# One block for the cross attention of prompt and sample tokens: 8 query tiles and 8 sequences taken in pairs

## The chip, the cores and the metric

The kernel runs on one core of a Trainium2 chip. The metric is device time in microseconds (us) of one execution. The engines spoken of are TensorE (PE, with its weight loads as PEld), VectorE (DVE), ScalarE (ACT), GpSimd (POOL) and SyncE (SP, which issues DMAs). TensorE's granted clock is given as a share of 2.4 GHz: 1.00 is 2.4 GHz, 0.50 is 1.2 GHz.

## What is computed

One step of a two-layer decoder in float32: layer 0 mixes with a convolution and latent attention, layer 1 with a state-space scan, and each layer ends in a gated cross attention. Only the cross attention matters here. It runs for 1024 prompt tokens against one memory of 256 tokens that the layer projects itself, and for 8 sequences of 4 sample tokens, each against its own cached memory of 256 tokens.

```python
def cross_attn(h, mk, mv, w_qg, w_o):
    b, t, _ = h.shape
    q, g = jnp.split(h @ w_qg, 2, axis=-1)
    q = q.reshape(b, t, X_HEADS, X_HEAD_DIM)            # 4 heads of 256
    s = jnp.einsum('bthd,bmhd->bhtm', q, mk).astype(F32) * (X_HEAD_DIM ** -0.5)
    p = jax.nn.softmax(s, axis=-1).astype(h.dtype)
    o = jnp.einsum('bhtm,bmhd->bthd', p, mv).reshape(b, t, D_MODEL)
    return (o * jax.nn.silu(g)) @ w_o
...
        xp = xp + rmsnorm(cross_attn(rmsnorm(xp, norm_pre_x[i]), mk, mv, x_w_qg[i], x_w_o[i]), norm_post_x[i])
        xs = xs + rmsnorm(cross_attn(rmsnorm(xs, norm_pre_x[i]), cache_mem_k[i], cache_mem_v[i],
                                     x_w_qg[i], x_w_o[i]), norm_post_x[i])
```

## The kernel before

The program is written engine by engine. A block holds one instruction stream for each engine; streams meet through semaphores inside a block and all engines meet at its end, so blocks run one after the other. `cross_attention` (L2257) runs once for each layer, as a row of such blocks: `memory_keys_values` projects the prompt's memory into KM (keys, transposed) and VM (values); `project` computes the transposed queries QT and the gate SGX = silu(g) for all 1056 tokens; `out_weights` (L453) is a block of SP alone that issues the load of the 4 MB output weights WO and of the gain gb; `cross_prompt`; `cross_sample`; and `out_project` (L463), which multiplies by WO in a three-product split, normalises and adds to X.

`cross_prompt` (L1987) takes the prompt in 8 tiles of 128 queries. For a tile PE computes the scores of 4 heads against 256 keys (`scores`, 8 matmuls of 256 columns, into one of two score tiles xS in PSUM), DVE takes the row maxima (L2044) and scales them (L2046), ACT takes the exponentials with their sums (L2080), DVE normalises (L2051, L2053), PE turns the probabilities into xT (`turn`, 8 transposes), and ACT copies them into HT (L2087), whose old content is no longer needed. After tiles 4 and 7, `values` makes the product with VM for 4 tiles at once, 16 matmuls of 512 columns with VM as weights, and DVE multiplies the result into SGX (L2061).

`cross_sample` (L2109) then takes the 8 sequences one by one. Two slots each hold 1 MB of cached keys (KB, loaded by SP) and values (VB, loaded by POOL), all four in HT; their first loads are issued at the start of this block, since HT was in use until then. For a sequence PE transposes the keys (`keys`, 16 transposes into four PSUM tiles ztp), DVE copies them out (L2195) into KM or VM, PE computes the scores of each head in its own 32-column tile of the array (L2154, both halves of one head in a row), DVE and ACT make the softmax as above, PE turns the probabilities (L2162), and `values` computes the output with VB as 16 full 128 x 128 weights and only 4 moving columns, those of the sequence's own tokens (L2171). DVE multiplies into SGX (L2213).

Matmuls of float32 stand as two records each in the trace, transposes as one. The records name tiles: xS, xT and xO are the prompt's scores, turned probabilities and outputs; ztp, zS, zPT and zO the sample's turned keys, scores, turned probabilities and outputs; WO_part, QT_part, KM_part and SGX_part are views of these buffers in `out_project`.

Of the kernel before, what the change touches and what calls it, by code (L numbers as in the profile page):

```python
# [51 lines left out]
def constants():  # L52
# [35 lines left out]
                            for t in range(16)], 1).astype(np.float32),  # L88
        "c_batch": (np.arange(SMP)[:, None] // TS == np.arange(NB)[None, :]).astype(np.float32),
# [38 lines left out]
def build(nc, A, O):  # L128
# [178 lines left out]
    def project(c, jobs, HT, HH, slots, extra=None, WH=None):  # L307
# [138 lines left out]
    y_w, y_g, y_mm, y_sq, y_ms, y_rs, y_sc, y_x = (sem(n) for n in (  # L446
        "yw_loaded", "ygain_loaded", "y_mm", "y_square", "y_ms", "y_rstd", "y_scaled", "x_updated"))
# [5 lines left out]
    def out_weights(c, W, gain):  # L453

        WO, gb = sb(c, "WO", [P, KT, D]), sb(c, "gb", [P, D])
        with nc.Block() as block:
            @block.sync
            def _(sp):
                sp.dma_start(WO[:], W.rearrange("(k p) n -> p k n", p=P)).then_inc(y_w, 16)
                sp.dma_start(gb[:], gain.partition_broadcast(P)).then_inc(y_g, 16)  # L460
        return WO, gb

    def out_project(YT, weights, WOH, YH, following=None, room=None):  # L463
# [17 lines left out]
        with ExitStack() as c:  # L481
# [55 lines left out]
            def _(act):  # L537
# [122 lines left out]
    s_cload, s_cl2, s_ctp, s_cev = layer_sem("conv_loaded"), sem("conv_w_loaded"), sem("conv_tp"), sem("conv_ev")  # L660
# [48 lines left out]
    s_new, s_sev, s_sout = layer_sem("state_gathered"), sem("state_ev"), sem("state_out")  # L709
# [417 lines left out]
    def mla_prompt(Q, QN, CKV, CKT, KRT, CV, SG, QLS, QRS):  # L1127
# [430 lines left out]
        layer_sem(n) if n != "cache_loaded" else [sem(f"cache_loaded{k}") for k in range(NCH)] for n in (  # L1558
# [347 lines left out]
    def memory_keys_values(l, KM, VM):  # L1906
# [74 lines left out]
        "x_scores", "x_negmax", "x_exp", "x_normed", "x_probs_tp", "x_probs_out", "x_pv", "x_pv_out"))  # L1981
    XSC = XD ** -0.5

    def cross_prompt(l, room, QT, KM, VM, SGX):

        n0 = NQ * l
        with ExitStack() as c:  # L1987
            PB = [sb(c, f"xPB{a}", [P, XH, MEM]) for a in range(2)]

            flat = room[:].rearrange("p k t -> p (k t)")  # L1990
            PT = [flat[:, a * XH * 1024:(a + 1) * XH * 1024].rearrange("p (h q) -> p h q", q=512) for a in range(2)]
            mx, nm, rsum, ri = (sb(c, n, [P, 2, XH]) for n in ("xmx", "xnm", "xrsum", "xri"))
            S = [pb(c, f"xS{a}", (P, XH * MEM)) for a in range(2)]
            TPp = pb(c, "xT", (P, XH * MEM))
            Op = [pb(c, f"xO{a}") for a in range(2)]
            block = c.enter_context(nc.Block())

            @block.tensor
            def _(pe):
                def scores(i):  # L2000
                    if i >= 2:
                        pe.wait_ge(x_ex, XH * (n0 + i - 1))
                    for h in range(XH):
                        for k in range(2):
                            m = nc.tensor.matmul(S[i % 2][:, h * MEM:(h + 1) * MEM], QT[:, 2 * h + k, i * P:(i + 1) * P],  # L2005
                                                 KM[:, 2 * h + k, :], start=k == 0, stop=k == 1)
                    m.then_inc(x_sc, 1)

                def turn(i):
                    pe.wait_ge(x_pn, n0 + i + 1)  # L2010
                    if i:
                        pe.wait_ge(x_te, n0 + i)
                    for h in range(XH):
                        for k in range(2):
                            t = nc.tensor.transpose(TPp[:, (2 * h + k) * P:(2 * h + k + 1) * P],
                                                    PB[i % 2][:, h, k * P:(k + 1) * P], ident[:])
                    t.then_inc(x_tp, 1)

                def values(half):
                    pe.wait_ge(x_te, n0 + 4 * (half + 1))  # L2020
                    for d in range(KT):
                        n = KT * half + d
                        if n >= 2:
                            pe.wait_ge(x_oe, 2 * n0 + n - 1)
                        for k in range(2):
                            m = nc.tensor.matmul(Op[n % 2][:], VM[:, k, d * P:(d + 1) * P], PT[half][:, (d // 2) * 2 + k, :],
                                                 start=k == 0, stop=k == 1)
                        m.then_inc(x_pv, 1)

                scores(0)  # L2030
                for i in range(NQ):
                    if i + 1 < NQ:
                        scores(i + 1)
                    turn(i)
                    if i == 4:
                        values(0)
                values(1)

            @block.vector
            def _(dve):  # L2040
                def maximum(i):
                    v = i % 2
                    dve.wait_ge(x_sc, n0 + i + 1)
                    dve_own.step(dve, nc.vector.tensor_reduce(mx[:, v, :], S[v][:].rearrange("p (h m) -> p h m", h=XH),  # L2044
                                                              AX.X, ALU.max))
                    nc.vector.tensor_scalar(nm[:, v, :], mx[:, v, :], -XSC, None, ALU.mult).then_inc(x_nm, 1)  # L2046

                def normalise(i):
                    v = i % 2
                    dve.wait_ge(x_ex, XH * (n0 + i + 1))  # L2050
                    dve_own.step(dve, nc.vector.reciprocal(ri[:, v, :], rsum[:, v, :]))  # L2051
                    for h in range(XH):
                        ins = nc.vector.tensor_scalar(PB[v][:, h, :], PB[v][:, h, :], ri[:, v, h:h + 1], None, ALU.mult)  # L2053
                    ins.then_inc(x_pn, 1)

                def outputs(half):
                    for d in range(KT):
                        n = KT * half + d
                        dve.wait_ge(x_pv, 2 * n0 + n + 1)
                        part = SGX[:, d, half * 512:(half + 1) * 512]  # L2060
                        nc.vector.tensor_tensor(part, part, Op[n % 2][:], ALU.mult).then_inc(x_oe, 1)  # L2061

                maximum(0)
                for i in range(NQ):
                    normalise(i)
                    if i + 1 < NQ:
                        maximum(i + 1)
                    if i == 4:
                        outputs(0)
                outputs(1)  # L2070

            @block.scalar
            def _(act):
                def exponent(i):
                    v = i % 2
                    act.wait_ge(x_nm, n0 + i + 1)
                    if i >= 2:
                        act.wait_ge(x_tp, n0 + i - 1)
# [18 lines left out]
    def cross_sample(l, room, KM, VM, QT, SGX):  # L2097
# [4 lines left out]
        with ExitStack() as c:  # L2102
# [35 lines left out]
            def _(pe):  # L2138
                def keys(b, s, step, meanwhile=None):
# [8 lines left out]
                    if meanwhile:  # L2148
                        meanwhile()
# [1024 lines left out]
```

## Time and profile before

| | before |
|---|---|
| median of 3 runs | 3289.17 us (3286.83 to 3292.13) |
| profiled execution | 3295.15 us, span 3293.5 us |
| PE busy | 2882.2 us (88%) |
| DVE, ACT, POOL busy | 1488.3, 765.9, 523.6 us |
| layer 0, `cross_prompt` and `cross_sample` | 1187.0 to 1356.3 us |
| layer 1, the same two | 3007.4 to 3177.5 us |

Since blocks follow one another, the time of a block is on the path that sets the end, whatever engine it waits for. Busy time of PE is no measure for the work left in it: records overlap, and at a granted clock of 0.50 the same work lasts twice as long. So this profile is read by block: from the first record of a block to the last, what one round of its loop costs, and at which clock.

### The profile page before, as it was taken

The page shows a single profiled execution, that of the slowest core. Times are in us where ns is not written, and L with a number is a line of the kernel's source. Part 1 is how long each engine was busy: PE and PEld are TensorE (multiplying, and loading weights), DVE is VectorE, ACT ScalarE, POOL GpSimd, SP SyncE. Part 2 cuts the span into 40 slices and gives each one's busy share as a digit, 9 for nine tenths or more (in the row PEclk, how much of TensorE's full clock was granted, in tenths as well). Part 3 has the DMA queues.
Part 4 walks back from the last instruction along what each step waited for, and adds up shares of the span by engine and source line. Part 5 has one row for each costly group of instructions (what it writes and reads, how often), then busy time and mean ns, then how long its engine had stood idle before and what let it go on. Part 6 is the DMA issues. An engine that isn't in the chain of part 4 may idle for free. (4 is left out here: it accounts for less than half of the span.)

```text
span 3293.5 us, 40266 instructions
## 1 busy us (share of the span) xinstructions
PE 2882.2 (88%) x16179; PEld 2278.4 (69%) x16179; DVE 1488.3 (45%) x2523; ACT 765.9 (23%) x1435; POOL 523.6 (16%) x422
## 2 busy tenths in 40 slices
PE   5999895997978998988997798758999977899899
PEld 5997564776758976768997576435555535798576
DVE  4997664663411023345655310557777631102333
ACT  3222352332202221223221211111121210223121
POOL 1012001431202200122121001012212210220011
PEclk9999898997988997798998899778998978899879
DMA  3111004660041114103221221663334103211321
GB/s 106 51 33 44 14 1 174 234 216 4 1 132 53 48 68 153 51 1 87 85 88 61 82 95 46 196 192 96 83 89 113 16 13 115 70 46 71 128 83 47
DMA packets 235057, 270.60 MB, mean 82 GB/s; under 512 B 35926, under 2 KB 190102, under 8 KB 229667
## 3 DMA queue, kind: packets, MB, share of 16 engines
q1 hardware_dynamic: 215074, 179.82, 18.1%
q0 software_dynamic: 16384, 75.77, 6.5%
q10 hardware_dynamic: 3456, 12.98, 1.0%
q8 instruction: 105, 1.72, 0.2%
q14 instruction: 38, 0.31, 0.0%
HBM read 226.64 MB, written 41.28 MB: 81 GB/s over the span
## 5 line engine op out<-in xcount | busy, mean ns | idle before, releaser
L305 PE MATMUL pp<-HH,WS_part 128*128 128x352 f32 x1776 | 575.4, 324 | 0.0
L303 PE MATMUL pp<-HH,WH 128*128 128x352 f32 x1344 | 437.3, 325 | 40.0 <-POOL WS_part L442 40.0
L304 PE MATMUL pp<-HT_part,WH 128*128 128x352 f32 x1344 | 435.3, 324 | 0.0
L305 PEld LDWEIGHTS pp<-HH,WS_part 128*128 128x128 f32 x1776 | 337.4, 190 | 0.0
L303 PEld LDWEIGHTS pp<-HH,WH 128*128 128x128 f32 x1344 | 255.1, 190 | 42.0 <-POOL WS_part L442 42.0
L2717 PE MATMUL OP<-oWO,YT 128*128 128x512 f32 (+1 forms) x576 | 255.9, 603 | 3.3 <-DVE XE L2844 3.3
L304 PEld LDWEIGHTS pp<-HT_part,WH 128*128 128x128 f32 x1344 | 255.2, 190 | 0.0
L442 POOL TENSOR_TENSOR WS_part<-WS,WH 128x1024 fp32r<-128x1024 f32 x56 | 144.1, 2573 | 649.5 <-ACT WH L393 649.5
L2717 PEld LDWEIGHTS OP<-oWO,YT 128*128 128x128 f32 (+1 forms) x576 | 104.9, 184 | 146.4 <-issue 142.8
L2044 DVE TENSOR_REDUCE xmx<-xS 128x4 f32<-128x1024 f32 x16 | 19.5, 1219 | 377.0 <-PE xS L2005 377.0
L993 DVE SCALAR_TENSOR_TENSOR CV<-GXP,cw,CV 128x512 f32<-128x512 f32 x240 | 161.9, 742 | 0.0
L303 PE MATMUL pp<-HH,CK_part 128*128 128x352 f32 x432 | 142.0, 329 | 7.9 <-DVE HT_part L858 7.9
L304 PE MATMUL pp<-HT_part,CK_part 128*128 128x352 f32 x432 | 140.5, 325 | 0.0
L303 PE MATMUL zp<-WZH,HH 128*128 128x512 f32 (+1 forms) x288 | 114.6, 398 | 14.5 <-ACT ZS L2555 14.0
L303 PE MATMUL yp<-QT_part,KM_part 128*128 128x512 f32 (+1 forms) x288 | 115.9, 402 | 12.6 <-DVE WO_part L601 12.6
L304 PE MATMUL yp<-WO_part,KM_part 128*128 128x512 f32 (+1 forms) x288 | 115.6, 401 | 0.0
L305 PE MATMUL yp<-QT_part,SGX_part 128*128 128x512 f32 (+1 forms) x288 | 114.5, 398 | 0.0
L305 PE MATMUL zp<-WZH,HT_part 128*128 128x512 f32 (+1 forms) x288 | 113.9, 396 | 0.0
L304 PE MATMUL zp<-WZ_part,HH 128*128 128x512 f32 (+1 forms) x288 | 113.6, 394 | 0.0
L2698 POOL TENSOR_TENSOR XK<-XK,Db 128x2048 f32<-128x2048 f32 (+1 forms) x9 | 88.1, 9785 | 139.0 <-DVE XD L2870 139.0
L2397 DVE SCALAR_TENSOR_TENSOR oACC<-EP,cwo,oACC 128x1024 f32<-128x1024 f32 x72 | 98.6, 1370 | 9.2 <-DVE oACC L2395 2.4
L2763 PE MATMUL U<-XD,CBt 128*128 128x64 f32 (+1 forms) x576 | 83.4, 318 | 16.5 <-DVE CBt L2876 9.4
(495 smaller groups left out, 5383.3 us busy)
## 6 DMA issues: line engine op xcount, KB each, us to landing
WS<-x_w_qg SPq DMA_DIRECT2D x32, 512.0 KB, 3.9
HT<-cache_mem_k SPq DMA_DIRECT2D x16, 1024.0 KB, 5.1
HT<-cache_mem_v POOLq DMA_DIRECT2D x16, 1024.0 KB, 5.4
CBt<-cum_scratch SPq DMA_DIRECT2D x8, 2048.0 KB, 10.2
xbc_scratch<-oACC ACTq DMA_DIRECT2D x24, 528.0 KB, 2.7
WS<-o_w_in SPq DMA_DIRECT2D x24, 512.0 KB, 3.7
XT<-xbc_scratch SPq DMA_DIRECT2D x8, 1536.0 KB, 7.6
WS<-e_w_in SPq DMA_DIRECT2D x18, 512.0 KB, 4.0
```

The lines of the kernel that those rows point to most:

```text
L303: nc.tensor.matmul(out, wh, xh, start=start, stop=False)
L304: nc.tensor.matmul(out, wh, xl, start=False, stop=False)
L305: return nc.tensor.matmul(out, wl, xh, start=False, stop=stop)
L442: nc.gpsimd.tensor_tensor(WL[:, k % slots, :, :], WS[:, k % slots, :, :], WH[k % 2][:, :, :], ALU.subtract).then_inc(p_lo, 1)
L993: ins = nc.vector.scalar_tensor_tensor(out=out, in0=src, scalar=tap, in1=out, op0=ALU.mult, op1=ALU.add)
L2044: dve_own.step(dve, nc.vector.tensor_reduce(mx[:, v, :], S[v][:].rearrange("p (h m) -> p h m", h=XH), AX.X, ALU.max))
L2397: ins = nc.vector.scalar_tensor_tensor(out=out, in0=src, scalar=tap, in1=out, op0=ALU.mult, op1=ALU.add)
L2698: nc.gpsimd.tensor_tensor(XK[R, :].rearrange("p (h e) -> p h e", h=SH), XK[R, :].rearrange("p (h e) -> p h e", h=SH), Db[R, :].unsqueeze(2 ...
L2717: m = nc.tensor.matmul(OP[hf][0:T, :], YT[:, k, 0:T], WO[:, k, hf * 512:(hf + 1) * 512], start=k == 0, stop=k == NX - 1)
L2763: m = nc.tensor.matmul(U[g % 2][R, e * SP_:(e + 1) * SP_], CB[R, h, R], XD[R, h * SP_:(h + 1) * SP_], start=True, stop=True)
```

## The change

One block, `cross_both`, takes the place of the blocks of `cross_prompt`, `cross_sample` and, in the cross attention, `out_weights`. Its loop takes query tile i together with sequence i.

- PE's order in round i: four times a head's prompt scores (2 matmuls) followed by 4 key transposes of sequence i into a single PSUM tile zT; the turn of tile i-1; the sample scores; four `values` columns of tile i-1; the sample values of sequence i-1; the other four `values` columns; the turn of the sample probabilities.
- Prompt `values` are made for each tile: 16 matmuls of 128 columns instead of 4 of 512 for each tile (16 for 4 tiles), into one PSUM tile xO. The prompt scores have one PSUM tile (before: two).
- Sample scores take the four heads alternately. Sample values now have the probabilities as weights of 32 columns, one column tile of the array for each head, and VB as 256 moving columns: 8 matmuls. They are summed over the sequences in PSUM, where rows of other sequences carry a probability of zero (`own`, a mask of 128 x 8 that DVE multiplies in with the normalisation). After the loop the sum is copied, turned and multiplied into SGX once.
- The scale of the scores goes into QT at the end of the projection, and the maximum comes out negated, so L2046 and L2202 have no successor.
- KB and VB lie in WO's buffer, and the turned keys, probabilities and their copies in HT. WO's four quarters are loaded when the last uses of these slots are done, the last one after the sample values of sequence 7. SP's queue at the block's start holds the keys of sequences 0 and 1, the mask, and gb.
- `out_weights` stays in layer 0's mixer with four DMAs of 1 MB instead of one of 4 MB, and `out_project` waits for the halves of WO separately.

```diff
 def out_project(...):  # ScalarE
-                act.wait_ge(y_w, w0 + 16)
+                act.wait_ge(y_w, 2 * w0 + 32)
                 for rows, cols in quarters:
+                    if rows.start:
+                        act.wait_ge(y_w2, 2 * w0 + 32)
                     nc.scalar.activation(WOH[:, rows, cols], WO[:, rows, cols], ACT.Copy).then_inc(y_wh, 1)
...
+    def cross_both(l, room, KM, VM, QT, SGX, WO, gb):
...
+            @block.sync
+            def _(sp):
+                w = A["x_w_o"][l].rearrange("(k p) n -> p k n", p=P)
+                for b in range(NB):
+                    if b >= 2:
+                        sp.wait_ge(z_tp, 4 * (n0 + b - 1))
+                    sp.dma_start(KB[b % 2], ck[:, b]).then_inc(z_l[b % 2], 16)
+                    if b == 1:
+                        sp.dma_start(own[:], A["c_batch4"]).then_inc(z_m, 16)
+                        sp.dma_start(gb[:], A["norm_post_x"][l].partition_broadcast(P)).then_inc(y_g, 16)
+                for a in range(2):
+                    sp.wait_ge(z_tp, 4 * (n0 + NB - 1 + a))
+                    sp.dma_start(WO[:, 2 * a:2 * a + 2, :], w[:, 2 * a:2 * a + 2, :]).then_inc(y_w, 16)
+                for a in range(2):
+                    sp.wait_ge(z_pv, n0 + NB - 1 + a)
+                    sp.dma_start(WO[:, 4 + 2 * a:6 + 2 * a, :], w[:, 4 + 2 * a:6 + 2 * a, :]).then_inc(y_w2, 16)
...
+                def values(i, a):
+                    pe.wait_ge(x_te, 2 * (n0 + i) + a + 1)
+                    if 2 * i + a:
+                        pe.wait_ge(x_oe, 2 * (n0 + i) + a)
+                    for d in range(4 * a, 4 * a + 4):
+                        for k in range(2):
+                            m = nc.tensor.matmul(OV[:, d % 4 * P:(d % 4 + 1) * P], VM[:, k, d * P:(d + 1) * P],
+                                                 PT[i % 2][:, d // 2 * 2 + k, :], start=k == 0, stop=k == 1)
+                    m.then_inc(x_pv, 1)
+                def sample_keys(b, q):
+                    if q == 0:
+                        pe.wait_ge(z_l[b % 2], 16 * (NB // 2 * l + b // 2 + 1))
+                    if 4 * b + q:
+                        pe.wait_ge(z_te, 4 * (n0 + b) + q)
+                    for k in range(2):
+                        for n in range(2):
+                            t = nc.tensor.transpose(KTp[:, (2 * k + n) * P:(2 * k + n + 1) * P],
+                                                    KB[b % 2][:, n, (2 * q + k) * P:(2 * q + k + 1) * P], ident[:])
+                    t.then_inc(z_tp, 1)
+                def sample_values(b):
+                    pe.wait_ge(z_pe, n0 + b + 1)
+                    pe.wait_ge(z_lv[b % 2], 16 * (NB // 2 * l + b // 2 + 1))
+                    for k in range(2):
+                        for h in range(XH):
+                            m = nc.tensor.matmul(OS[32 * h:32 * h + 32, 0:XD], PZT[b % 2][:, k, 32 * h:32 * h + 32],
+                                                 VB[b % 2][:, k, h * XD:(h + 1) * XD], start=b == 0 and k == 0,
+                                                 stop=b == NB - 1 and k == 1, tile_position=(0, 32 * h), skip_group_check=True)
+                    m.then_inc(z_pv, 1)
+                for i in range(NQ + 1):
+                    for h in range(XH):
+                        if i < NQ:
+                            scores(i, h)
+                            sample_keys(i, h)
+                    if i:
+                        turn(i - 1)
+                    if i < NQ:
+                        sample_scores(i)
+                    if i:
+                        values(i - 1, 0)
+                        sample_values(i - 1)
+                        values(i - 1, 1)
+                    if i < NQ:
+                        sample_turn(i)
...
+                dve.wait_ge(z_m, 16 * (l + 1))
+                for i in range(NQ + 1):
+                    if i < NQ:
+                        for q in range(4):
+                            sample_keys_out(i, q)
+                        maximum(i)
+                        sample_maximum(i)
+                    if i:
+                        outputs(i - 1, 0)
+                    if i < NQ:
+                        sample_normalise(i)
+                        normalise(i)
+                    if i:
+                        outputs(i - 1, 1)
...
-            out_w = out_weights(c, A["x_w_o"][l], A["norm_post_x"][l])
-            cross_prompt(l, HT, QT, KM, VM, SGX)
-            cross_sample(l, HT, KM, VM, QT, SGX)
+            WO, gb = sb(c, "WO", [P, KT, D]), sb(c, "gb", [P, D])
+            cross_both(l, HT, KM, VM, QT, SGX, WO, gb)
```

On PE, a tile of the prompt before stands as scores and turn, with nothing between:

```order
L2005 MATMUL xS_1<-KM,QT 128x256 [waits x_exp]
L2005 MATMUL xS_1<-KM,QT 128x256 x7
L2015 MATMUL xT<-ident,xPB_1 128x128 [waits x_probs_out,x_normed]
L2015 MATMUL xT<-ident,xPB_1 128x128 x7
L2005 MATMUL xS_1<-KM,QT 128x256 [waits x_exp]
```

On PE after, one round of the loop (its first two key quarters left out) holds the prompt's scores and key transposes in turn, then the rest of both kinds of tokens:

```order
L2052 MATMUL xS<-KM,QT 128x256 x2
L2088 MATMUL zT<-ident,WO 128x128 [waits z_k_out]
L2088 MATMUL zT<-ident,WO 128x128 x3
L2065 MATMUL xT_1<-ident,HT 128x128 [waits x_normed]
L2065 MATMUL xT_1<-ident,HT 128x128 x7
L2099 MATMUL zS<-HT,QT 32x256 [waits z_probs_out,z_k_out]
L2099 MATMUL zS<-HT,QT 32x256 x7
L2076 MATMUL xO<-HT,VM 128x128 [waits x_probs_out]
L2076 MATMUL xO<-HT,VM 128x128 x7
L2114 MATMUL zO<-WO,PZT_1 32x256 [waits memv_slot0,z_probs_out]
L2114 MATMUL zO<-WO,PZT_1 32x256 x7
```

Every key quarter now waits until DVE has emptied the one zT tile, and between two such quarters PE has a head's prompt scores to do.

On SP, at the start of the cross attention's block of the changed kernel, what the queue holds:

```order
L2025 DMA WO<-cache_mem_k 128x2x1024 x2
L2027 DMA xown<-c_batch 128x8
L2028 DMA gb<-norm_post_x 128x1024
L2025 DMA WO<-cache_mem_k 128x2x1024 [waits z_k_tp] x6
L2032 DMA WO<-x_w_o 128x2x1024 [waits z_k_tp] x2
L2035 DMA WO<-x_w_o 128x2x1024 [waits z_pv] x2
```

And on DVE of the changed kernel, its first instructions in that block:

```order
L2161 COPY HT<-zT 128x512 [waits z_k_tp,z_mask]
L2161 COPY HT<-zT 128x512 [waits z_k_tp] x3
L2143 TENSOR_REDUCE xnm<-xS 128x4 [waits x_scores]
L2167 TENSOR_REDUCE znm<-zS 128x1 [waits z_scores]
```

DVE's first copy waits for the mask, which stands in SP's queue behind 2 MB of keys.

## Rows read from the trace of the kernel before

**Rows 1.** Timeline, block borders, layer 0: start us, duration us, engine, line, what
```profile
1184.86 0.46 ACT L2270 ACTIVATE SGX<-pp 128x352 f32<-128x352 f32 x1 [3.35 <-PE pp L305]
...
1187.02 7.14 PE L2005 MATMUL xS<-KM,QT 128*128 128x256 f32 x32 [2.19 <-PEq L456]
...
1356.12 0.19 DVE L2213 TENSOR_TENSOR SGX<-SGX,zO 128x32 f32<-128x32 f32 x1 [8.26 <-PE zO L2171]
...
1357.57 7.29 ACT L548 ACTIVATE QT_part<-WO 128x2048 fp32r<-128x2048 f32 x4
...
1362.40 0.77 PE L303 MATMUL yp<-QT_part,KM_part 128*128 128x512 f32 x1 [6.32 <-DVE WO_part L601]
```
**Rows 2.** Timeline, layer 1: first and last record of the two blocks
```profile
3007.36 5.81 PE L2005 MATMUL xS<-KM,QT 128*128 128x256 f32 x18 [2.54 <-PEq L456]
...
3177.27 0.19 DVE L2213 TENSOR_TENSOR SGX<-SGX,zO 128x32 f32<-128x32 f32 x1 [8.27 <-PE zO L2171]
```
**Rows 3.** Stretches: length, busy PE, PEld, DVE, ACT, POOL (records), PEclk, DMA share, GB/s
```profile
1187.00:1266.30 79.30, 67.33 (x256) 44.23 (x256) 32.08 (x72) 24.13 (x73) 0.00 (x0) 0.94 0.15 60
1266.30:1356.40 90.10, 83.02 (x528) 70.61 (x528) 31.45 (x72) 7.58 (x24) 5.82 (x8) 0.68 0.52 187
```
**Rows 4.** Timeline, one prompt tile in the first of the two blocks
```profile
1195.44 1.22 DVE L2044 TENSOR_REDUCE xmx<-xS 128x4 f32<-128x1024 f32 x1
1195.58 1.09 PE L2015 MATMUL xT<-ident,xPB 128*128 128x128 f32 x8 [1.42 <-DVE xPB L2053]
1196.51 3.62 PE L2005 MATMUL xS<-KM,QT 128*128 128x256 f32 x16
...
1197.63 0.47 ACT L2080 ACTIVATE xPB<-xS,xnm 128x256 f32<-128x256 f32 x1
...
1199.81 1.14 DVE L2053 TENSOR_SCALAR xPB<-xPB,xri 128x256 f32<-128x256 f32 x4
```
**Rows 5.** Timeline, one sequence in the second block
```profile
1296.39 3.65 PE L2145 MATMUL ztp<-ident,HT 128*128 128x128 f32 x16
...
1302.23 4.38 PE L2171 MATMUL zO<-PZT,HT 128*128 x32
...
1306.47 3.65 PE L2145 MATMUL ztp<-ident,HT 128*128 128x128 f32 x16
```
**Rows 6.** Stretches of half a microsecond inside that sequence
```profile
1304.50:1305.00 0.50, 0.50 (x7) 0.50 (x6) 0.00 (x0) 0.00 (x0) 0.00 (x0) 1.00 0.04 16
...
1306.00:1306.50 0.50, 0.50 (x4) 0.50 (x4) 0.00 (x0) 0.00 (x0) 0.00 (x0) 0.50 0.00 0
```
**Rows 7.** Layer 0's latent attention on sample tokens: timeline, then the stretch around it
```profile
599.71 1.53 PE L1653 MATMUL KTp<-ident,HT 128*128 128x128 f32 x12
601.07 1.02 PE L1660 MATMUL Sc<-RTs,QD 128*128 128x512 f32 x2
...
603.34 1.08 PE L1686 MATMUL Op<-HT,PCT 128*32 128x128 f32 x32
604.24 1.04 PE L1666 MATMUL Sc<-QN,DTt_part 128*32 128x512 f32 x8
605.21 0.98 PE L1653 MATMUL KTp<-ident,HT 128*128 128x128 f32 x7
...
598.00:606.00 8.00, 8.00 (x113) 5.63 (x106) 4.79 (x10) 2.52 (x5) 3.57 (x7) 1.00 0.67 250
```
**Rows 8.** Layer 1's scan, full-width weights with 64 moving columns: timeline, then its stretch
```profile
2229.16 7.06 PE L2763 MATMUL U<-XD,CBt 128*128 128x64 f32 x32 [1.67 <-DVE Y L2892]
...
2229.00:2236.00 7.00, 6.84 (x32) 6.87 (x33) 1.30 (x3) 0.00 (x0) 0.38 (x1) 0.50 0.00 0
```
**Rows 9.** Start of the sample block: timeline, then landing of the 16 key loads
```profile
1271.41 3.41 PE L2145 MATMUL ztp<-ident,HT 128*128 128x128 f32 x16 [5.86 <-DMA HT<-cache_mem_k]
1272.57 0.69 DVE L2195 COPY KM<-ztp 128x512 f32<-128x512 f32 x1 [6.29 <-PE ztp L2145]
...
DMA to landing us min/median/max: 4.7/5.1/9.3
```

More of the change, by code:

```diff
@@ L1995, in cross_prompt @@
[L1995 to L2070, printed above, removed]
@@ L2092, in build @@
[L2092 to L2108 removed]
+            KBT = [flat[:, a * 2048:(a + 1) * 2048].rearrange("p (k m) -> p k m", m=MEM) for a in range(2)]
@@ new lines, in scores, with turn @@
+                def scores(i, h):
+                    if h == 0 and i:
+                        pe.wait_ge(x_ex, n0 + i)
+                    for k in range(2):
+                        m = nc.tensor.matmul(S[:, h * MEM:(h + 1) * MEM], QT[:, 2 * h + k, i * P:(i + 1) * P],
+                                             KM[:, 2 * h + k, :], start=k == 0, stop=k == 1)
+                    if h == XH - 1:
+                        m.then_inc(x_sc, 1)
+                def turn(i):
+                    pe.wait_ge(x_pn, n0 + i + 1)
+                    for a in range(2):
+                        if i:
+                            pe.wait_ge(x_te, 2 * (n0 + i - 1) + a + 1)
+                        for h in (2 * a, 2 * a + 1):
+                            for k in range(2):
+                                t = nc.tensor.transpose(TPp[a][:, (2 * (h % 2) + k) * P:(2 * (h % 2) + k + 1) * P],
+                                                        PB[i % 2][:, h, k * P:(k + 1) * P], ident[:])
+                        t.then_inc(x_tp, 1)
@@ L2176, in _ @@
-                keys(0, 0, 0)
-                keys(1, 1, 0, lambda: turned(0, 0))
-                values(0, 0, 0)
-                with loop(pe, 0, NB // 2 - 1) as j:
-                    for s in range(2):
-                        keys(2 * j + 2 + s, s, j + 1, lambda: turned(2 * j + 1 + s, 1 - s))
-                        pe.wait_ge(z_oe, n0 + 2 * j + s + 1)
-                        values(2 * j + 1 + s, 1 - s, j + s)
-                turned(NB - 1, 1)
-                pe.wait_ge(z_oe, n0 + NB - 1)
@@ new lines, in sample_turned @@
+                def sample_turned(b):
+                    act.wait_ge(z_pt, n0 + l + b + 1)
+                    if b >= 2:
+                        act.wait_ge(z_pv, n0 + b - 1)
+                    nc.scalar.activation(PZT[b % 2][:], SS[:, MEM:2 * MEM].rearrange("p (k q) -> p k q", k=2), ACT.Copy).then_inc(z_pe, 1)
+                for i in range(NQ + 1):
+                    if i:
+                        turned(i - 1, 0)
+                        turned(i - 1, 1)
+                    if i < NQ:
+                        exponent(i, 0)
+                        exponent(i, 1)
+                        sample_exponent(i)
+                        exponent(i, 2)
+                        exponent(i, 3)
+                        sample_turned(i)
```

221 lines of the change are left out of this document (95 added, 126 removed).

## The prediction

> **What bounds the kernel now.** Blocks follow one another, so I first read the borders in the timeline. In layer 0 the projection's last gate copy ends at 1185.32 us (1184.86 + 0.46), the prompt block's first matmul starts at 1187.02, and the sample block's last multiplication ends at 1356.31 [rows 1]: 171.0 us. In layer 1 the two blocks take 170.1 us [rows 2], with the same 1.7 us ahead of them 171.8. The change touches these 342.8 us and hardly more.
>
> Then the busy time by stretch. The prompt block takes 79.3 us at a granted clock of 0.94, the sample block 90.1 us at 0.68 [rows 3]. Neither is full in its own way. In a prompt tile PE has 0.93 us of transposes and 3.6 us of scores and otherwise waits for the chain maximum, four exponentials, normalisation [rows 4]: latency. In a sequence PE is never idle, one comes every 10.08 us [rows 5], but the output matmuls with 4 moving columns hold it for 4.2 us, and behind them the clock has fallen from 1.00 to 0.50 [rows 6], so that 16 transposes take about 3.4 us.
>
> **The new round, PE's work.** At clock 1.00, start to start:
> - prompt scores, 16 records: 3.45 us (3.62 with the last one's tail) [rows 4];
> - turn of a tile, 8 transposes: 0.93 [rows 4];
> - 16 key transposes: 12 take 1.36 us, so 0.113 each, 1.8 [rows 7];
> - sample scores: 16 records of 256 columns in alternating 32-column tiles. The nearest row has 8 of 512 columns, as many columns in all: 0.97 [rows 7];
> - sample values are the same shape: 0.97;
> - prompt values: 32 records of 128 columns with full-width weights. This shape doesn't stand in the trace by itself. Below, a transpose has such a weight load and 128 columns in 0.113 us; above, load and matmul would not overlap, 0.107 + 0.107 us. With 64 columns at clock 0.50, 32 records take about 6.9 us, 0.215 each, although the columns alone would add 0.107 to a load of 0.214 if the two excluded one another [rows 8]. They overlap, so I take the transpose's 0.113: 3.6 us;
> - turn of the sample probabilities: 0.23.
>
> Sum 12.0 us.
>
> A rule speaks against the many shapes in a round. The Trainium skill, TensorEngine Tiling (Array Packing), Key Properties, states that changing the tiling mode drains TensorE. A round has four such changes, a sequence before had two. The row shows little of it: the 8 tiled records of rows 7 take 0.97 us where a quarter of 8 x 0.43 (twice a 256-column record's 0.216) is 0.86, so at most 0.11 for a drain, 0.22 us more a round and some 4 us in all; 0.97 already holds half of that.
>
> **The new round, waits.** I walk through one from PE's first score at 0. A head's scores and a key quarter take 0.86 + 0.45; 0.3 us after a quarter's transposes DVE starts its copy, which takes 0.69 (four transposes at clock 0.50 take 0.85 from 1271.41, the copy starts at 1272.57) [rows 9]. The next head's scores hide 0.86 of the 1.05 us, so each of three quarters waits 0.2: the last ends at 5.8, its copy at 6.8. The turn of the tile before fills 5.8 to 6.7; the sample scores wait 0.1, and end at 7.8; four value columns until 9.6, sample values until 10.6, the other value columns wait 0.1 for the one xO tile and end at 12.5, the sample's turn at 12.7. So a round takes **12.8 us**.
>
> Is anything else later? DVE takes the maximum (1.22) from 6.8 to 8.0, the sample's to 8.5, ACT's five exponentials of 0.45 us run from 8.1 to 10.5 with the wait for the sample's maximum hidden. The next scores need the one score tile empty: 10.5 against 12.8, slack 2.3. DVE normalises until 12.6 (0.7 for the output, 0.5 and 1.3 for the two), and is free when the next quarter comes at 14.4. DVE works 8.1 us of the round, ACT about 5. The DMAs bring 2 MB a round, less dense than the 2 MB in 10.08 us before [rows 5]; a slot has over 10 us for a median landing of 5.1 us [rows 9]. The removed L2046 and L2202 (under 0.2 us each) lie in hidden time: nothing.
>
> **First and last round.** The keys are fetched only when the block starts, as before; PE waited 5.86 us and went on at 4.9 us after the issue, at half clock (3.41 us for 16 transposes) [rows 9]. Now DVE's first copy also waits for the mask, which is queued on SP behind the second sequence's keys. The slowest key load, the second of a pair, landed after 9.3 us [rows 9]; it is issued 0.4 us after the first, so the mask comes at about 10.2 and PE's second quarter starts at 10.95. Who waits: PE, with everything behind it. Three more head scores and quarters, partly at half clock, end near 15.8, the copy at 16.8, maxima at 18.5, exponentials at 20.5: the first round takes **21 us** (16.5 if the mask comes with the first keys). The last one: turn 0.9, copy by ACT, values from 1.5 to 3.3, sample values to 4.3, values to 6.2, output 7.2, copy, turn, two small multiplications: **8.6 us**.
>
> WO's last quarter is issued at 4.6 in that round and lands at 9.7 by the median. ACT needs it about 3.3 us after the block's end at 8.6 (0.3 us border, then the gate's split and one quarter; this is 1357.57 + 1.9 against 1356.31 in rows 1). The slack is 2.2 us, so nothing; with a landing of 9.3 us it costs 2.0 us a layer.
>
> **The sum.** A layer: 0.3 (an ordinary border, as at 1356.31; SP's block of its own is gone) + 21 + 7 x 12.8 + 8.6 = 119.5 us. Two layers 239.0 against 342.8: 103.8 us less. The mixer's three more DMA issues, about 0.43 us each in a block of SP alone, give back 1.3. Against the profiled execution: 3295.15 - 102.5 = 3192.7. That execution lies 6.0 us above the median of the runs, so for the median **3186.7 us**.
>
> Bounds: a round of 12.0 (no wait) and a first round of 16.5 give 5.6 + 4.5 us less a layer: 3166. If each of PE's 11 waits in a round costs a full hand-off of 0.3 us, a round takes 15.3; with 3 us more in the first and 2 us for WO that is 22.5 us more a layer, 3232.
>
> **Rivals.**
> - *Hand-offs bound, not PE.* One score tile, one xO and one zT tie PE, DVE and ACT together. For it: in the prompt block such a chain sets the time already [rows 4]. Against: the slack of 2.3 us. Rounds of 15.3 us: 3222 to 3235.
> - *The value columns cost twice*, 0.213 us a record: 3.2 us x 8 rounds x 2 layers more, 3238. Against it stands rows 8.
> - *The clock stays as in the sample block.* At 0.68 a round takes 12.0 / 0.68 + 0.8 = 18.4 us, 39 us more a layer: 3265. For it: half of the work comes from there. Against: before the fall PE did matmuls of 4 columns, which are gone, and a stage of transposes, tiled and full matmuls runs at 1.00 [rows 7]. The Trainium skill, TensorE: Matmul & The Clock Gate, Part 4, holds that transposes don't count as busy for the clock; the trace doesn't bear that out at 601.07, where they fill most of the time before and the clock is 1.00.
> - *Slower than before.* The one mechanism that reaches this is the clock: with rounds of (171.4 - 0.3 - 29.6) / 7 = 20.2 us all gain is gone, that is from a mean clock of 12.0 / 19.4 = 0.62 downwards. The place is the loop, whose every round holds a few waits of PE; in the first round PE idles over 3 us twice, and a fall like that of rows 9 would have to last. At 0.50 throughout, rounds of 24.8 us give 84 + 9 us more a layer: 3373.
> - *It doesn't overlap*: PE's in-order stream makes the pair of a tile and a sequence as long as the two were. 79.3 / 8 + 10.1 = 20.0 us [rows 3, 5] a round, and the time is unchanged. The walk excludes it.
>
> **How the numbers follow.** Forecast 0.72 (3166 to 3222), hand-offs 0.10, value columns 0.04, clock at 0.68 0.08, slower 0.03, no overlap 0.01, below 3166 0.02. The range takes the first two: 3166 to 3235. A measurement tells about 0.2% (6.6 us) from no change. Faster 0.96, within 0.2% 0.01, slower 0.03.
>
> **What the changed profile would show.** Starts of the maximum L2143 every 12.8 us at a clock of 0.95 or more; DVE's first copy near 10 us after the block's start, released by a DMA; 32 xO records in 3.6 us; no idle time of ACT in `out_project` released by WO's load. I am wrong if L2143 comes every 15 us with PE idle before xS (hand-offs), if xO's records stand 0.2 us apart, or if PEclk in the loop is under 0.8.

## The result, and the profile after it

| | before | after |
|---|---|---|
| median of 4 runs each, same chip | 3290.65 us (3286.83 to 3293.24) | 3190.12 us (3189.32 to 3191.76) |
| profiled span | 3293.5 us | 3187.7 us |
| layer 0, gate's end to `out_project` | 171.3 us | 122.3 us |
| layer 1, the same | 172.4 us | 119.5 us |

The ratio is 0.9698, with a 95% interval of 0.9684 to 0.9712: faster, 3.4 us above the forecast of 3186.7. The last two rows of the table are taken from the end of the projection's last gate copy to ACT's first split of SGX in `out_project` (KM_part), so that the border is in; they are used below for every kernel. Together they lost 101.9 us. One single run of the kernel before, beside the last pair of experiments, took 4331.69 us at a mean clock of 0.63 and is left out of every comparison.

The page of the changed kernel begins with its span and the busy times:

```profile
span 3187.7 us, 40235 instructions
PE 2791.4 (88%) x16311; PEld 2213.6 (69%) x16311; DVE 1485.6 (47%) x2481; ACT 767.1 (24%) x1451; POOL 520.1 (16%) x422
```

PE's share is 88% as before, so it tells nothing of the change. The stretches tell more (length, busy PE, PEld, DVE, ACT, POOL, granted clock, DMA share, GB/s): layer 0's whole block, its steady rounds, and the beginning of its second round.

```profile
1189.40:1311.10 121.70, 109.07 (x850) 85.13 (x850) 61.12 (x123) 32.16 (x105) 5.83 (x8) 0.92 0.49 177
1220.00:1300.00 80.00, 80.00 (x683) 62.73 (x684) 47.67 (x94) 26.49 (x90) 4.29 (x6) 1.00 0.48 170
1211.50:1217.50 6.00, 6.00 (x22) 4.90 (x20) 2.41 (x7) 0.38 (x1) 0.00 (x0) 0.56 0.00 0
```

Before, the two stretches ran at 0.94 and 0.68 [rows 3]. Now 80 us of rounds run at 1.00, and PE's records leave no gap there. The borders of the block, beside [rows 1], from the timeline of layer 0:

```profile
1188.67 0.46 ACT L2256 ACTIVATE SGX<-pp 128x352 f32<-128x352 f32 x1 [3.35 <-PE pp L306]
...
1189.44 1.10 PE L2052 MATMUL xS<-KM,QT 128*128 128x256 f32 x4 [0.81 <-PEq L2260]
...
1302.75 1.04 PE L2065 MATMUL xT<-ident,HT 128*128 128x128 f32 x8
...
1310.66 0.48 DVE L2195 TENSOR_TENSOR SGX<-SGX,zS 128x128 f32<-128x128 f32 x2 [0.53 <-PE zS L2136]
...
1311.44 1.06 ACT L546 ACTIVATE KM_part<-SGX 128x1024 fp32r<-128x1024 f32 x1 [6.97 <-PEq L2000]
...
1312.41 7.29 ACT L553 ACTIVATE QT_part<-WO 128x2048 fp32r<-128x2048 f32 x4
```

ACT's split of WO (L553) follows its split of SGX without a gap: the late load of WO costs nothing. The last round, from 1302.75 to 1311.14, takes 8.4 us.

One steady round in the timeline, to be read beside [rows 4] and [rows 5]; it goes from the score at 1233.28 to the one at 1245.95:

```profile
1233.12 1.21 DVE L2143 TENSOR_REDUCE xnm<-xS 128x4 f32<-128x1024 f32 x1
1233.28 1.07 PE L2099 MATMUL zS<-HT,QT 128*32 128x256 f32 x16
1234.28 2.05 PE L2076 MATMUL xO<-HT,VM 128*128 128x128 f32 x16
...
1236.26 1.07 PE L2114 MATMUL zO<-WO,PZT 128*32 128x256 f32 x16
...
1237.26 2.05 PE L2076 MATMUL xO<-HT,VM 128*128 128x128 f32 x16
...
1239.15 0.38 PE L2106 MATMUL zS<-ident,PZ 128*128 128x128 f32 x2
...
1239.37 1.03 PE L2052 MATMUL xS<-KM,QT 128*128 128x256 f32 x4
...
1240.67 1.03 PE L2052 MATMUL xS<-KM,QT 128*128 128x256 f32 x4
1240.87 0.69 DVE L2161 COPY HT<-zT 128x512 f32<-128x512 f32 x1 [0.83 <-PE zT L2088]
1241.62 0.66 PE L2088 MATMUL zT<-ident,WO 128*128 128x128 f32 x4
1242.11 1.03 PE L2052 MATMUL xS<-KM,QT 128*128 128x256 f32 x4
...
1244.98 1.04 PE L2065 MATMUL xT<-ident,HT 128*128 128x128 f32 x8
...
1245.79 1.22 DVE L2143 TENSOR_REDUCE xnm<-xS 128x4 f32<-128x1024 f32 x1
1245.95 1.07 PE L2099 MATMUL zS<-HT,QT 128*32 128x256 f32 x16
```

The round takes 12.67 us. Start to start, it is sample scores 1.00, values 1.98, sample values 1.00, values 1.89, the sample's turn 0.22, four heads with their key quarters 5.61, the tile's turn 0.97. The first quarter of the four takes 1.30, those that wait for DVE's copy 1.44 (1240.67 to 1242.11); the 0.14 us between them shows only from start to start, since the modelled ends of the records cover it. The two column-tiled groups take 1.00 us each at four tiles of 32 columns; the output by 4 moving columns took 4.2 us in [rows 5].

The first round, beside [rows 9], on PE and DVE:

```profile
1194.24 1.12 PE L2088 MATMUL zT<-ident,WO 128*128 128x128 f32 x4 [3.69 <-DMA WO<-cache_mem_k]
1195.15 1.92 PE L2052 MATMUL xS<-KM,QT 128*128 128x256 f32 x4
1200.37 0.69 DVE L2161 COPY HT<-zT 128x512 f32<-128x512 f32 x1 [192.09 <-DMA xown<-c_batch]
1201.12 1.11 PE L2088 MATMUL zT<-ident,WO 128*128 128x128 f32 x4 [4.05 <-DVE HT L2161]
...
1211.58 1.91 PE L2052 MATMUL xS<-KM,QT 128*128 128x256 f32 x4
...
xown<-c_batch SPq DMA_DIRECT2D x1, 4.0 KB, 10.0
```

DVE's copy waits for the mask (xown), which lands 10.0 us after its issue (the last row is from the DMA issues of that stretch: size, us to landing). PE stands for 4.05 us behind it. The scores of the next heads run at half clock (1.92 us for 4 records instead of 1.03), and so does the start of the second round at 1211.58, at 0.56 in the stretch above.

### The profile page after: what moved, and what is told of

Its sections match the earlier page's. It is cut to its first block and busy times, and to the rows that moved or that the text cites. A ratio compares the mean times of both kernels' runs of the same rounds, so it can differ in the third digit from the quotient of the medians.

```text
span 3187.7 us, 40235 instructions
## 1 busy us (share of the span) xinstructions
PE 2791.4 (88%) x16311; PEld 2213.6 (69%) x16311; DVE 1485.6 (47%) x2481; ACT 767.1 (24%) x1451; POOL 520.1 (16%) x422
## 5 line engine op out<-in xcount | busy, mean ns | idle before, releaser
L2161 DVE COPY HT<-zT 128x512 f32<-128x512 f32 x64 | 44.2, 691 | 437.1 <-DMA xown<-c_batch 383.6
L1732 DVE COPY QN<-KTp 128x512 f32<-128x512 f32 x128 | 82.7, 686 | 27.6 <-PE KTp L1658 27.6
## 6 DMA issues: line engine op xcount, KB each, us to landing
CBt<-cum_scratch SPq DMA_DIRECT2D x8, 2048.0 KB, 10.1
```

Source lines behind the costliest of these rows:

```text
L1732: nc.vector.tensor_copy(KTs[:, r, :], KTp[r % 3][:]).then_inc(d_kte, 1)
L2161: nc.vector.tensor_copy(KBT[b % 2][:, 2 * q:2 * q + 2, :], KTp[:].rearrange("p (k m) -> p k m", k=2))\
```

## Experiments

All of them change `cross_both`, but for one that starts from the kernel before. The kernel before was run beside each; its single runs there lie between 3275.6 and 3308.6 us, so small differences are read from the profiled stages as well.

**The mask ahead of the keys**

```diff
             def _(sp):
+                sp.dma_start(own[:], A["c_batch4"]).then_inc(z_m, 16)
                 for b in range(NB):
...
                     if b == 1:
-                        sp.dma_start(own[:], A["c_batch4"]).then_inc(z_m, 16)
```

> The mask is loaded first on SP's queue, ahead of both key loads; nothing else differs from the changed kernel (3190.1 us). Theory (DVE's first copy waits for the mask, and the mask for the second sequence's keys): the first copy starts about 6 us after the block's start instead of 10.9, the first round takes 17.5 us instead of 22.1, the rounds after it 12.68 as before; 3181 us. Rival (the copy waits, but the second sequence's keys or the half clock decide when the second round starts): the first copy moves and the second round's first scores don't; 3190 us.

Measured: 3178.43 us (3170.74 to 3187.84, 6 runs), ratio to before 0.9655 (0.9622 to 0.9687). From its timeline, the first round:

```profile
1182.15 1.10 PE L2052 MATMUL xS<-KM,QT 128*128 128x256 f32 x4 [0.81 <-PEq L2260]
1187.38 1.07 PE L2088 MATMUL zT<-ident,WO 128*128 128x128 f32 x4 [4.13 <-DMA WO<-cache_mem_k]
...
1188.57 0.69 DVE L2161 COPY HT<-zT 128x512 f32<-128x512 f32 x1 [186.52 <-PE zT L2088]
...
1189.96 1.05 PE L2088 MATMUL zT<-ident,WO 128*128 128x128 f32 x4
...
1194.54 1.21 DVE L2143 TENSOR_REDUCE xnm<-xS 128x4 f32<-128x1024 f32 x1
```

The copy is released by PE's transposes. The mask now lands 1.5 us after its issue instead of 10.0, as the trace of its loads tells:

```profile
DMA to landing us min/median/max: 1.5/1.5/1.5
```

The first maximum starts 12.4 us after the first score instead of 18.2 (12.8 instead of 17.9 in layer 1). The next maximum comes 11.6 and 11.7 us later, as changed 12.8 and 10.2: this span depends on how much of the second round's start runs at half clock, here 2.6 us in layer 0 and a little more in layer 1, as changed 5.1 and none. The layers take 115.4 and 115.8 us, 10.6 us less together than the changed kernel's 241.8. The wait for the mask is a cost of its own, on the path of the block. The first copy starts 6.4 us after the first score, as the theory said (about 6).

Since the intervals of the two kernels' ratios touch, they were run once more, side by side on one chip:

> The changed kernel itself, beside the version with the mask first on the same chip, since the times of one kernel on different chips differ by more than the effect in dispute. By the theory its first maximum stands 18.3 to 18.6 us after the loop's first score and the median is 9 to 11 us above the version with the mask first; if that version's gain was a matter of the chip or of the run, the two agree within 3 us.

> The mask's load stands ahead of the keys on SP's queue, all else is the changed kernel, run on the same chip. By the theory (one latency in each layer's first round, 5.3 us a layer) 9 to 11 us less than the changed kernel here, ratio to the kernel before 0.003 lower than the changed kernel's. Rival: the clock's course elsewhere gives it back, under 5 us less.

Measured: 3187.24 us (3182.51 to 3193.98, 5 runs; ratio 0.9684, 0.9655 to 0.9712) as changed and 3182.73 us (3172.93 to 3192.25, 6 runs; 0.9667, 0.9640 to 0.9695) with the mask first. In the profiled runs the first maximum stands 17.5 and 18.4 us after the first score as changed, 13.0 and 12.7 us with the mask first; the layers take 240.5 and 231.9 us together, the spans are 3180.8 and 3171.3. So the stages differ by 8.7 us, a little under what was expected (in layer 0 as changed the clock came back earlier than in the first profile, by the fourth head's scores), and the profiled spans by 9.5, but the medians by only 4.5: less than the theory asked for, within the rival's "under 5 us", and inside the scatter of 11 and 19 us between single runs. The rival's mechanism isn't seen in the two profiled runs, which differ by only 0.8 us outside the two stages. What is shown is the gain in the stage, twice, in both layers. In the whole time it isn't shown clear of noise: the medians differ by 4.5 us here and by 11.7 in the first set, and in both sets the intervals of the ratios overlap.

**The turn among the key quarters**

```diff
                         if i < NQ:
                             scores(i, h)
+                        if i:
+                            turn(i - 1, h)
+                        if i < NQ:
                             sample_keys(i, h)
-                    if i:
-                        turn(i - 1)
```

(`turn` takes two transposes of one head at a time.)

> The turn of a prompt tile is cut into four pairs of transposes, one behind each head's scores and ahead of the key quarter, so that PE has 1.09 us of work instead of 0.86 while DVE empties the one zT tile. Theory (three key quarters of a round wait about 0.13 us each): rounds of 12.3 us instead of 12.68, 5 us less in all, 3185 us. Rival (DVE's normalisation of the tile before ends at the round's end, so an earlier turn waits for it): rounds of 12.7 us or more, 3190 us or slower, with PE idle before xT instead of before zT.

Measured: 3193.54 us (3186.89 to 3202.88, 4 runs), ratio 0.9698 (0.9657 to 0.9739). The ratio is the changed kernel's, so the whole time doesn't tell the two apart; the stages do. The rounds grew from 12.68 to 13.12 us, and the layers take 124.3 us each, 6.9 more together. In its timeline:

```profile
1240.40 1.03 PE L2052 MATMUL xS<-KM,QT 128*128 128x256 f32 x4
...
1241.92 1.03 PE L2052 MATMUL xS<-KM,QT 128*128 128x256 f32 x4
...
1243.64 0.69 DVE L2162 COPY HT<-zT 128x512 f32<-128x512 f32 x1 [0.83 <-PE zT L2088]
1244.39 1.07 PE L2099 MATMUL zS<-HT,QT 128*32 128x256 f32 x16 [0.78 <-DVE HT L2162]
```

The wait between quarters is gone: 1.52 us is 0.86 for the scores, 0.22 for two transposes and 0.44 for the four. But PE now stands for 0.78 us before the sample scores, until the last quarter's copy is done. In the changed kernel the tile's turn stands in that gap and fills it. The edit moved the filler to where 0.14 us a quarter was to be had, and opened a gap of 0.78. Neither of my expectations named this. The rival's number came (rounds of 12.7 us or more), but not its place: PE stands before zS and not before xT. The theory counted the three waits and forgot what the turn hid.

**Both edits**

> Two edits of the changed kernel: mask loaded first, and the turn of a prompt tile woven into the key quarters. Each alone is expected to save 9 and 5 us. If they are independent their gains add: 3176 us. If the first round's clock carries over, the sum differs by more than 3 us from that.

Measured: 3187.75 us (3182.45 to 3193.98, 5 runs), ratio 0.9682 (0.9658 to 0.9705). Rounds 13.12 us, layers 118.3 and 119.2, together 4.2 us less than as changed; 10.6 less for the mask and 7 x 0.44 x 2 = 6.2 more for the turn give 4.4. The expected 3176 us took the turn for a gain; what the expectation asked, whether the two add, holds in the stages. The medians can't show so small a sum.

**The heads of the column tiles in a row**

```diff
-                    for k in range(2):
-                        for h in range(XH):
+                    for h in range(XH):
+                        for k in range(2):
```

(in the sample scores and in the sample values; the accumulation over k is the same)

> The sample scores and sample values take one head after the other, both halves of a head in a row, as the sample scores did before the change. Theory (neighbouring matmuls run at the same time only in different column tiles): zS and zO take 1.8 to 1.9 us each instead of 1.0, rounds of 14.4 us, 27 us more: 3217 us. Rival (the 32-column form alone makes them short): no change, 3190 us.

Measured: 3194.11 us (3187.14 to 3199.65, 4 runs), ratio 0.9693 (0.9652 to 0.9733). Rounds 12.72 us, and both groups 1.09 us instead of 1.07:

```profile
1240.10 1.09 PE L2099 MATMUL zS<-HT,QT 128*32 128x256 f32 x16
...
1243.11 1.09 PE L2114 MATMUL zO<-WO,PZT 128*32 128x256 f32 x16
```

So the alternation, which the change brought to the scores and which I held for needed, gives 0.04 us a round. The groups are short in either order of the heads, 16 records in 1.07 or 1.09 us, where 16 full-width records of as many columns take 3.62 us [rows 4]. Both orders have the tiles of 32 columns in common; what inside the array makes them overlap isn't shown.

**The sample's outputs as before, in the new loop**

```diff
-                    for k in range(2):
-                        for h in range(XH):
-                            m = nc.tensor.matmul(OS[32 * h:32 * h + 32, 0:XD], PZT[b % 2][:, k, 32 * h:32 * h + 32],
-                                                 VB[b % 2][:, k, h * XD:(h + 1) * XD], ...)
+                    for d in range(KT):
+                        h = d // 2
+                        for k in range(2):
+                            m = nc.tensor.matmul(OS[:, d * TS:(d + 1) * TS], VB[b % 2][:, k, d * P:(d + 1) * P],
+                                                 PZT[b % 2][:, k, b * TS + 32 * h:b * TS + 32 * h + TS],
+                                                 start=k == 0, stop=k == 1)
```

(DVE multiplies into SGX after each sequence, and the copy, the turn and the two multiplications at the end are gone)

> In the merged loop the sample values are made as before the change: 16 full weights and 4 moving columns for each sequence, multiplied into SGX for each sequence; the sum over sequences and its last turn are gone. Theory A (the 4-column matmuls pull the clock down, wherever they stand): zO 3.5 us or more at a mean clock of 0.75 to 0.9 in the loop, rounds of 16.5 to 18 us, 3250 to 3280 us. Theory B (in the merged loop they are too small a share for the clock to fall): clock 1.00, rounds of 15.2 us, 3228 us.

Measured: 3259.19 us (3242.71 to 3264.85, 4 runs), ratio 0.9882 (0.9837 to 0.9927). The layers take 148.5 and 148.7 us. Most rounds take 16.7 us, one in each layer 15.05 (and one, the second, 18.3). The timeline shows the output matmuls of a usual round (from 1238.37) and of the short one (from 1255.09), and two stretches show the clock behind each:

```profile
1238.37 3.63 PE L2117 MATMUL zO<-PZT,WO 128*128 128x4 f32 x32
1241.86 2.72 PE L2076 MATMUL xO<-HT,VM 128*128 128x128 f32 x16
...
1244.80 1.84 PE L2052 MATMUL xS<-KM,QT 128*128 128x256 f32 x4
...
1255.09 3.63 PE L2117 MATMUL zO<-PZT,WO 128*128 128x4 f32 x32
1258.58 2.03 PE L2076 MATMUL xO<-HT,VM 128*128 128x128 f32 x16
...
1242.00:1248.00 6.00, 6.00 (x32) 5.19 (x32) 1.48 (x3) 0.38 (x1) 0.71 (x1) 0.72 0.55 175
1255.00:1262.00 7.00, 7.00 (x62) 6.85 (x61) 3.19 (x10) 1.06 (x5) 0.71 (x1) 1.00 0.30 97
```

The outputs take 3.49 us (1238.37 to 1241.86) instead of 1.00. After them the clock is 0.72 in most rounds and 1.00 in the short one: of the 4.0 us that a usual round is longer, 2.4 are the shape itself (the short round against 12.68) and 1.6 the clock behind it (16.70 against 15.05).

**The new outputs of the samples in the old block**

From the kernel before: `cross_sample` with the probabilities as 32-column weights, the mask, the sum over the sequences in PSUM and one multiplication at the end. The prompt's block, `out_weights` and the order stay. The loops over pairs of sequences are written out, since the positions of start and stop depend on the sequence.

```diff
-                    for d in range(KT):
-                        h = d // 2
-                        for k in range(2):
-                            m = nc.tensor.matmul(Op[:, d * TS:(d + 1) * TS], VB[s][:, k, d * P:(d + 1) * P], ...)
+                    for k in range(2):
+                        for h in range(XH):
+                            m = nc.tensor.matmul(Op[32 * h:32 * h + 32, 0:XD], PZT[s][:, k, 32 * h:32 * h + 32],
+                                                 VB[s][:, k, h * XD:(h + 1) * XD], start=b == 0 and k == 0, ...)
```

> The kernel before (3290.7 us) with one part of the change: sample values in the new form (probabilities as 32-column weights, cached values as 256 moving columns, summed over the sequences, mask loaded first), in its own block behind the prompt's, its loop written out. Theory A (the form and the clock it pulled down are most of the gain): a sequence takes about 6 us instead of 10.08 at a clock above 0.9, 3226 us, which leaves some 36 us to the merging. Theory B (the clock stays at 0.68 since the transposes are what pulls it down): a sequence takes 8 us, 3257 us, and the merging carries two thirds.

Measured: 3225.79 us (3211.58 to 3227.93, 4 runs), ratio 0.9786 (0.9754 to 0.9818). Two sequences' key transposes and a stretch of the sample block:

```profile
1285.92 1.97 PE L2148 MATMUL ztp<-ident,HT 128*128 128x128 f32 x16
...
1291.39 1.97 PE L2148 MATMUL ztp<-ident,HT 128*128 128x128 f32 x16
...
1275.00:1310.00 35.00, 34.27 (x293) 25.03 (x292) 22.94 (x50) 5.30 (x17) 3.57 (x5) 0.94 0.95 357
```

A sequence takes 5.5 us instead of 10.1 [rows 5], at a clock of 0.94 instead of 0.68 [rows 3]; the 0.94 holds the block's start at half clock, and from 1279 to 1310 us it is 1.00. The layers take 137.0 and 136.9 us, 273.9 together, which is 69.8 of the 101.9 us. So with the form of the sample's outputs changed first, two thirds of the gain are that form, with the clock that it brings back, and the merging of the two loops adds the last third, 32.1 us.

The split depends on the order, which the experiment before this one shows. There the loops are merged with the old outputs, and the layers take 297.2 us: the merging alone gives 46.6 us, and the form on top of it 55.4. Each part alone gives more than it adds to the other, 69.8 and 46.6 against a sum of 101.9. What holds in both orders is that the form is the larger part. The loop written out is in the 69.8 too and wasn't tried by itself.

Alone, the new form runs at a DMA share of 0.95, while the merged loop asks for the same bytes at a share of 0.48. So there is little room left for the loads below 5.5 us a sequence. That they already set the pace isn't shown: PE's long waits for keys, 7.2 us in all, lie at the block's start.

## Why the prediction came out right

- **The round.** 12.8 us forecast, 12.68 measured. The terms are right one by one to within 0.3 us: 3.87 us for the prompt's values (3.6 forecast), 1.00 for each column-tiled group (0.97), 0.97 for the turn with its wait (0.93 and 0.1) and 5.61 for scores and key quarters (5.8). That the sum is closer than its terms is in part luck: the values were taken 0.27 us too short and the quarters 0.2 too long. The waits of the key quarters were taken too large, 0.2 instead of 0.14 us: DVE starts its copy 0.2 us after PE has gone on to the next score (1240.67 to 1240.87, at full clock), and the 0.3 was read from a stretch at half clock. The 0.113 us for a value record came out at 0.118 to 0.124 (1.89 and 1.98 us for 16).
- **The clock.** Forecast 0.95 or more, measured 1.00 in the rounds. What took it down before were the outputs with 4 moving columns and full-width weights. Two experiments show this from both sides: put back into the new loop they bring stretches at 0.72, and taken out of the old block they lift it from 0.68 to 0.94. The Trainium skill (TensorE: Matmul & The Clock Gate, Part 4) lets transposes not count as busy; here every round of 12.68 us holds 26 of them in some 2.9 us, and the clock stays at 1.00, so the trace doesn't bear out that they cost it at this share. A stage of transposes alone isn't among the runs.
- **Changes of tiling.** The rule that I weighed against the change (the Trainium skill, TensorEngine Tiling (Array Packing), Key Properties: a change of mode drains TensorE) allowed 0.22 us more a round. Over the 0.97 of the forecast the two groups of a round took 0.06. A tiled group takes 1.00 us with both its changes, 0.14 over the 0.86 that I worked out as its share without a drain. What of this is a drain isn't told apart from its start and tail.
- **The first round.** 21 us forecast, 22.1 and 21.6 measured (1189.44 to 1211.58, and 2954.75 to 2976.38 in layer 1). The mechanism and place were right: the mask's issue comes 0.9 us after the block's start and it lands 10.0 us later, so DVE's copy starts 10.9 us after PE's first score; I had put the landing at 10.2, with the 9.3 us of the slowest key load. Putting the mask first was worth 4.5 us a layer by the prediction, and 5.3 and 4.3 in the two pairs of runs.
- **The second round**, which I took for an ordinary one, is the step with the largest error: 15.1 us in layer 0 (1211.58 to 1226.69) and 12.8 in layer 1 (2976.38 to 2989.16). PE idles for 2.22 us behind the probabilities at the end of the first round, and in layer 0 it then goes on at half clock for 5.1 us, in layer 1 at full clock. I had put half clock into the first round alone. The same wait of 2.2 us stands in both layers of the other three profiles (the second one as changed and the two with the mask first), and from the first maximum to the second it is 10.2 to 11.8 us there, against 12.8 and 10.2 in the first profile. So what follows the wait costs between nothing and 2.5 us, and what decides it isn't shown.
- **The last round**, 8.6 forecast and 8.4 measured, and WO's load, hidden as forecast.
- **The sum.** 119.5 a layer against 122.0 and 119.2, counted as in the prediction to DVE's last multiplication. Before it was 171.0 and 172.1 (not 171.8: the gate's copy of layer 1 ends at 3005.3), so 101.9 us less instead of 103.8. That the median came within 3.4 us of the forecast is closer than the forecast can claim: run again, the same kernel had a median of 3187.24 us with single runs from 3182.51 to 3193.98, and the parts of the program outside the stages differ by several us from run to run, as shown below.
- **The mixer.** The 1.3 us for three more DMA issues are not to be seen. From the end of DVE's last multiplication of that part to DVE's first work with a loaded constant in the next it is 16.0 us before and 15.8 after:

```profile
534.12 0.69 DVE L1540 TENSOR_TENSOR SG<-SG,OB 128x512 f32<-128x512 f32 x1 [2.15 <-PE OB L1349]
...
550.78 0.17 DVE L1714 TENSOR_SCALAR pt<-pt_i 128x8 f32<-128x8 int32 x1 [15.98 <-DMA own<-c_own]
```

```profile
534.13 3.62 PE L1354 MATMUL OB<-RG,V 128*64 128x128 f32 x32 [0.88 <-DVE RG L1538]
...
537.78 0.69 DVE L1545 TENSOR_TENSOR SG<-SG,OB 128x512 f32<-128x512 f32 x1 [3.80 <-PE OB L1354]
...
538.74 2.00 SPq L462 DMA_DIRECT2D WO<-e_w_out  x4
...
554.30 0.17 DVE L1719 TENSOR_SCALAR pt<-pt_i 128x8 f32<-128x8 int32 x1 [15.83 <-DMA own<-c_own]
```

The four issues stand there (2.00 us), but what the next part waits for is a small load (own from c_own) that SP issues behind these 4 MB, at 550.43 us, and that lands 3.8 us later. I had costed the issue and not asked who waits for what. That this part starts 3.7 us later than before is not shown to be the change. Of the 3.7 us, 2.0 were there before the 32 output records L1354 began, and 1.65 are these records, which took 3.62 us at half clock in this execution and 1.97 before. They took 1.97 us also in the second profile of the changed kernel and in both with the mask first.

Differences outside the changed blocks are also most of what is left between stages and totals. Between the two layers' cross attentions the changed kernel was 5.7 us shorter (1643.3 against 1649.0), before the first one 3.8 longer, after the second 1.9 shorter. With the 101.9 us this makes up the 105.8 between the spans. The 5.7 us are no gain of the change that these runs could show: from `out_project`'s first split in layer 0 to the gate's end in layer 1, the profiles of kernels that differ in the cross attention's loop alone lie between 1640.4 us (the turn among the quarters) and 1660.3 us (the old outputs), with the kernel before at 1648.7.

**The rivals.** Hand-offs don't bound: in the steady rounds PE waits only 0.14 us at three quarters and some 0.04 at the turn, and ACT's last exponential, with the read of its sum, ends at 1236.76, 2.6 us before the next scores at 1239.37. The value columns don't cost twice. The mean clock of the whole block was 0.92 in layer 0; a fall like the one to 0.56 at the second round's start didn't last.

## What to carry to other kernels

- Read from a block's timeline what the expensive shape does to the clock of the work behind it. Replacing matmuls with 4 moving columns by column-tiled ones with 256 gave 69.8 us of this gain by itself and 55.4 on top of the merged loop, and in the merged loop 1.6 of 4.0 us a round lay in other instructions.
- When PE's order is changed, list for each piece the gap that it fills now. Moving 0.9 us of transposes away from a gap of 0.8 us cost more than three small waits of 0.14 were worth.
- A small load that the first step of a block needs goes ahead of the large ones on its queue: one line, 4.3 to 5.3 us in the stage of each layer. The version with the mask first had the lower median in both sets of runs, though over the changed kernel the gain in the whole time isn't clear of noise.

## What the runs showed of the hardware that I had not expected

- Groups of 32-column tiles overlap even where both matmuls for the same tile stand in a row: 16 records in 1.09 us instead of 1.07 with alternating tiles, where as many full-width records take 3.62 us.
- With the outputs by 4 moving columns, two rounds of equal instructions differ by 1.65 us (16.70 and 15.05): in one the clock falls behind them, in the other it stays at 1.00. The same pattern comes in both layers, in the same round.
- A load of 4 KB landed 10.0 us after its issue behind 2 MB on the same queue, and 10.1 and 10.7 in the second profile. Put first on the queue it landed after 1.5 to 1.7 us.
